# A decoder block's first stage with the contraction outside: features-first input, upper value tiles normalised late, the row factor through DRAM

## The chip, the cores and the metric

The kernel runs on one core of a Trainium2 chip. The metric is the device time of one execution in microseconds (us), as a median over repeated executions. The core has TensorE (PE: matmuls, and PEld: weight loads), VectorE (DVE), ScalarE (ACT), GpSimd (POOL) and SyncE (SP), which here only issues DMAs.

## The reference, cut to what matters

```python
h = rms_norm(x, norm1_g[l])                          # x: 1 x 1024 x 1024, float32
proj = jnp.einsum('bsd,dc->bsc', h, w_in[l])         # 1024 features -> q, k, v, pool, gates
q = proj[..., :c_q];  k = proj[..., c_q:c_k]         # 512 columns each
v = proj[..., c_k:c_v].reshape(B, S, 4, 128)         # 512 columns
...
q = rms_norm(q, q_norm_g[l]);  k = rms_norm(k, k_norm_g[l])
a = diff_attention(q, k, v, lam)                     # causal, 4 heads, two softmaxes a head
...                                                  # pooling mixer, gates, output projection
x = x + jnp.einsum('bsd,de->bse', merged, w_o[l])
u = jnp.square(jax.nn.relu(jnp.einsum('bsd,df->bsf', rms_norm(x, norm2_g[l]), w_mlp_in[l])))
x = x + jnp.einsum('bsf,fd->bsd', u, w_mlp_out[l])
```

`rms_norm` divides each row of x by the root of the mean of its squares (the reciprocal is called the row factor below) and multiplies each feature by its gain. There is one layer.

## The kernel before, in words

Every large product is done in three matmuls: both operands are split into a rounded part and the rest (`_hi` by a copy on ACT, `_lo` by a subtraction on DVE), and hi·hi, lo·hi and hi·lo are summed in PSUM (`passes`, L2299). One step of a contraction is thus three matmuls of 128x128 by 512 columns.

The first stage makes h transposed (`featT`, features on partitions, 8 blocks of 128 features by 1024 tokens, hi and lo), and from it v for all eight token tiles (`v_tok`). It goes token tile by token tile. For tile t: SP loads `x_tile` (128 tokens x 1024, L587); ACT squares it with a sum over the row (`x_square`, L1024); POOL turns the sum into the row factor (`inverse_root`, L948, two instructions); DVE multiplies by the factor and the gain (`x_norm`, L1507); PE transposes eight 128x128 blocks (`x_transpose`, L2312); ACT and DVE split them (`x_hi`, `x_lo`); PE multiplies with the value weights `v_w`, 24 matmuls (`v_project`, L2477; for tile 0 `v_first`); ACT and DVE split the result (`v_hi_part`, `v_lo_part`). The gain, one row, is spread over the partitions by matmuls with a single contraction row (L2506).

Two query-key projections follow among the last value tiles (`project`, 24 matmuls each, after tiles 5 and 6). Their rows are squared and copied by ACT (`qk_take`), summed (`qk_sum`), given a factor by POOL (`qk_inverse`), normalised (`qk_norm`), transposed on PE (`qk_transpose`, L2366) and split (`qk_hi`, `qk_lo`). Then the attention stage starts: `attend(0)` does three steps of the pool projection and then `scores(0)` (L2403, matmuls at L2422), which needs the split query and key tile 0. From there on PE has an order of work written out by hand, in which projections fill the places between the attention products, and later the gates, the output projection and the MLP follow.

Each engine runs its own list in the written order and waits on semaphores. SP's list is: x tile 0 in two halves, the value weights in four loads (`load_v_w`, L589), x tiles 1 and 2 among them, seven small loads for the vectors (L629 to L635), x tiles 3 and 4, the first query-key weights (`load_qk`, eight loads of 256 KB), x tiles 5 to 7, two loads for the pool projection.

Of the kernel before, what the change touches and what calls it, by code (L numbers as in the profile page):

```python
# [34 lines left out]
def trunk_layer(nc, x, norm1_g, w_in, b_gate, q_norm_g, k_norm_g, lam_params, subln_g,  # L35
                pool_w, pool_scale, w_up_attn, w_up_pool, w_o, norm2_g, w_mlp_in, w_mlp_out, y):
# [33 lines left out]
    with ExitStack() as ctx:  # L70
# [22 lines left out]
        g1_row = at("g1_row", 144, [P, D])  # L93
        h_row = [at(f"h_row{i}", 148 + 4 * i, [P, D]) for i in range(2)]
        square1 = at("square1", 156, [P, D])
        g_one = at("g_one", 208, [1, D])
# [7 lines left out]
        x_tile = [at(f"x_tile{i}", 128 + 4 * i, [P, D]) for i in range(4)]  # L104
        prob = [at(f"prob{c}", 144 + 4 * c, [P, SEQ]) for c in range(2)]
        w_tok = [at(f"w_tok{i}", 152 + 4 * i, [P, SEQ]) for i in range(2)]
        qk_square = [at(f"qk_square{i}", kb, [P, 8, HEAD]) for i, kb in enumerate((158, 118))]
# [85 lines left out]
        gate_store = nc.dram_tensor("gate_store", [2 * GP, P, SEQ], F32, kind="Internal").ap()  # L193
        res_store = nc.dram_tensor("res_store", [T, P, D], F32, kind="Internal").ap()
# [14 lines left out]
        vec_rows = at("vec_rows", 218, [N_ROWS, P])  # L209
# [9 lines left out]
        x_ss_half = sm(11)  # L219
# [22 lines left out]
        def sem(name):  # L242
# [4 lines left out]
        x_in = [sem(f"x_in{i}") for i in range(4)]  # L247
        res_in = [sem(f"res_in{i}") for i in range(3)]
# [5 lines left out]
        o_in = [[sem(f"o_in{i}_{j}") for j in range(4)] for i in range(2)]  # L254
        vec_in, g1_ready, g_in, x0_in, y_out = sem("vec_in"), sem("g1_ready"), sem("g_in"), sem("x0_in"), sem("y_out")

        zeroed, const_ready = sem("zeroed"), sem("const_ready")
        vec_full, col_ready, lam_step, lam_exped = (sem(n) for n in ("vec_full", "col_ready", "lam_step", "lam_exped"))

        w_hi, w_ready = sem("w_hi"), sem("w_ready")  # L260
        v_full, v_hi, v_ready = sem("v_full"), sem("v_hi"), sem("v_ready")

        x_squared, x_mean, x_inv, h_ready, xT_full, xT_hi, xT_split = (sem(n) for n in (
            "x_squared", "x_mean", "x_inv", "h_ready", "xT_full", "xT_hi", "xT_split"))
# [23 lines left out]
        gate_in = [sem(f"gate_in{i}") for i in range(4)]  # L288
# [73 lines left out]
        def qk_w(h2, piece):  # L362

            return (4 if h2 == 0 else 10) + piece + 1

        def x_w(g):

            return (9, 10, 15, 16)[g]
# [28 lines left out]
        def x_bank(t, b):  # L397

            return 2 * (t % 2) + b

        def v_bank(t):

            return POOLED + t % 2

        FIRST_W = 4 * HEADS + 1
# [75 lines left out]
        RAW_LOADS = (10, 10, 4, 4)  # L481
# [85 lines left out]

        def o_source(n):
# [14 lines left out]
        def _(sp):  # L583
            def load_x(t):

                wait(sp, h_ready, t - 2 if t > 3 else 0)
                sp.dma_start(x_tile[t % 4][:], x_rows[t]).then_inc(x_in[t % 4], 16)  # L587

            def load_v_w(i):  # L589

                src = w_in_v[:, 2 * i:2 * i + 2, V0:V0 + HEADS * P]
                sp.dma_start(k4(raw[i][:], 2), src).then_inc(raw_in[i], 16)
# [6 lines left out]
            def load_qk(h2, piece):  # L599

                r = piece if h2 == 0 else piece % 2
                sp.wait_ge(w_ready, piece + 1 if h2 == 0 else (9, 10, 11, 12)[piece])
# [5 lines left out]
            def load_pool_w(g):  # L608

                c0 = X0 + (GROUPS - 1 - g) * P  # L610
                load(g % 2, w_in_v[:, :, c0:c0 + P], (5, 6, 13, 14)[g], KD)
# [7 lines left out]
            sp.dma_start(x_tile[0][:, LOW], x_rows[0][:, LOW]).then_inc(x0_in, 16)  # L619
            sp.dma_start(x_tile[0][:, HIGH], x_rows[0][:, HIGH]).then_inc(x_in[0], 16)  # L620
            load_v_w(0)
            load_v_w(1)
            load_v_w(2)
            load_x(1)
            load_v_w(3)
            load_x(2)

            rows_of = lambda v: v.rearrange("l (j p) -> (l j) p", p=P)
            sp.dma_start(vec_rows[BG:PS, :], rows_of(b_gate)).then_inc(vec_in, 16)  # L629
            sp.dma_start(vec_rows[PS:SG, :], rows_of(pool_scale)).then_inc(vec_in, 16)  # L630
            sp.dma_start(vec_rows[SG:SG + 1, :], subln_g).then_inc(vec_in, 16)
            for r, g in ((QG, q_norm_g), (KG, k_norm_g)):
                for c in range(2):
                    sp.dma_start(vec_rows[r:r + 1, c * HEAD:(c + 1) * HEAD], g).then_inc(vec_in, 16)
# [3 lines left out]
            load_x(3)  # L638
            load_x(4)
            for piece in range(4):  # L640
                load_qk(0, piece)
            load_x(5)
            load_x(6)
            load_x(7)
# [18 lines left out]
            for p in range(4):  # L663
                if p == 2:
                    sp.wait_ge(pooled_full, 2 * GROUPS)
                load(p, gate_cols(2 * p, P), (15, 16, 16, 16)[p], KD)
# [168 lines left out]
            sp.dma_start(g2_row[:], norm2_g.to_broadcast([P, D])).then_inc(g_in, 16)  # L835
# [100 lines left out]
        def _(pool):  # L936
# [18 lines left out]
            def x_inverse(t, squared, mean, inv):  # L955
                inverse_root(x_ss[:, t:t + 1], D, x_ms[:, t:t + 1], x_rstd[:, t:t + 1], 1, squared, t + 1, mean, t + 1, inv)
# [26 lines left out]
            pool.wait_ge(x_squared, 1)  # L983
# [32 lines left out]
        def _(act):  # L1016
# [29 lines left out]
            def qk_hi(n):  # L1046

                act.wait_ge(tb_full, TB_USE["qk", n])
                if n == 0:
                    act.wait_ge(col_ready, 3)  # L1050
# [1708 lines left out]
```

## Time and profile before

| | |
|---|---|
| median of 3 runs | 1250.77 us (1250.71 to 1251.3) |
| span of the profiled execution | 1249.3 us |
| PE busy | 1240.8 us, 99% of the span |
| DVE busy | 937.9 us, 75% |
| ACT busy | 556.4 us, 45% |
| POOL busy | 141.4 us, 11% |
| DMA | 169.75 MB, mean 136 GB/s |
| first matmul of scores(0) | 76.32 us after the span's start |

The profiled execution has a span of 1249.3 us, from its first to its last instruction; the runs take 1.5 us more around it (1250.77 less 1249.3). Busy time of PE is a union of matmuls whose ends are modelled, and consecutive matmuls overlap: a row of 0.39 us for one matmul does not mean that it takes 0.39 us of the engine's time; the distance between starts tells that.

### The profile page before, as it was taken

The numbers are of one execution on the slowest core, as the hardware profiler recorded it, in microseconds if no ns is written. First come the engines' busy times: TensorE is split into PE (matmuls) and PEld (weight loads), VectorE is DVE, ScalarE is ACT, GpSimd is POOL, SyncE is SP. The second block draws the span as 40 slices with busy tenths as digits, with TensorE's granted clock in tenths as the row PEclk, the third lists the DMA queues.
The fourth block names the chain that finished last, engine by engine and source line by source line (L and its number), as shares of the span: only waits on it lengthen the run. The fifth ranks groups of instructions, "written<-read, shape, count | busy, mean of one in ns | idle before, by whom it ended". The sixth has DMA issues, their size and how long they took to land.

```text
span 1249.3 us, 16209 instructions
## 1 busy us (share of the span) xinstructions
PE 1240.8 (99%) x5885; PEld 1022.0 (82%) x5885; DVE 937.9 (75%) x1316; ACT 556.4 (45%) x961; POOL 141.4 (11%) x198
## 2 busy tenths in 40 slices
PE   9999999999999999999999999999999999999999
PEld 6878888887788888888887888888888888888887
DVE  5547786778987778754688778778679988879764
ACT  5436665666553324322345545445445333333330
POOL 2113223223300040000000000000000000000035
PEclk9999999999999999999999999999999999999999
DMA  7100120103375457332213553453569644363223
GB/s 274 35 17 16 58 60 19 38 23 106 127 261 177 144 188 267 119 117 86 100 65 129 170 175 123 160 173 112 176 240 363 218 158 167 102 236 102 101 95 141
DMA packets 110354, 169.75 MB, mean 136 GB/s; under 512 B 5806, under 2 KB 55875, under 8 KB 110276
## 3 DMA queue, kind: packets, MB, share of 16 engines
q1 hardware_dynamic: 110274, 168.72, 39.5%
q8 instruction: 47, 0.77, 0.2%
q14 instruction: 31, 0.25, 0.1%
q10 hardware_dynamic: 2, 0.00, 0.0%
HBM read 118.37 MB, written 50.33 MB: 135 GB/s over the span
## 4 chain that ended last, share of the span: by engine, by line
PE 89%; DVE 5%; ACT 3%; issue 2%; DMA 1%; SPq 0%; POOL 0%; ACTq 0%; DVEq 0%
PE bank L2301 81%; PE bank L2443 2%; PE bank L2422 2%; PE bank L2381 1%; DVE slot_lo L1504 1%; DMA x_tile<-in_x 1%; DVE c L2201 1%; DVE pair_lo L2095 1%; PE bank L2372 1%; PE bank L2658 1%; DVE small L1587 1%; DMA gate_store<-out_tile 1%; PE bank L2319 0%; ACT slot_hi L1022 0%; ACT prob L1067 0%
## 5 line engine op out<-in xcount | busy, mean ns | idle before, releaser
L2301 PE MATMUL bank<-o_hi,s_lo 128*128 128x512 f32 (+1 forms) x452 | 175.0, 387 | 0.0
L2301 PE MATMUL bank<-o_hi,s_hi 128*128 128x512 f32 (+1 forms) x452 | 175.0, 387 | 0.0
L2201 DVE TENSOR_TENSOR c<-bank,c 128x512 f32<-128x512 f32 x112 | 75.7, 688 | 35.6 <-PE bank L2301 33.9
L2301 PE MATMUL bank<-featT_hi,pair_hi 128*128 128x512 f32 x256 | 99.9, 390 | 0.7 <-DVE c L2201 0.6
L2301 PE MATMUL bank<-o_lo,s_hi 128*128 128x512 f32 (+1 forms) x260 | 100.3, 386 | 0.0
L2301 PE MATMUL bank<-featT_lo,pair_hi 128*128 128x512 f32 x256 | 99.6, 389 | 0.0
L2301 PE MATMUL bank<-featT_hi,pair_lo 128*128 128x512 f32 x256 | 99.6, 389 | 0.0
L2301 PEld LDWEIGHTS bank<-o_hi,s_hi 128*128 128x128 f32 x452 | 84.9, 188 | 17.5
L2301 PEld LDWEIGHTS bank<-o_hi,s_lo 128*128 128x128 f32 x452 | 84.9, 188 | 17.2
L1472 ACT ACTIVATE s_hi<-s_raw 128x2048 fp32r<-128x2048 f32 x28 | 53.7, 1917 | 94.6 <-DMA s_raw<-u_store 94.6
L1448 ACT ACTIVATE c<-c 128x512 f32<-128x512 f32 x64 | 39.9, 624 | 118.8 <-DVE c L2201 118.8
L2145 DVE TENSOR_TENSOR s_lo<-s_raw,s_hi 128x2048 fp32r<-128x2048 f32 x28 | 65.7, 2345 | 22.6 <-ACT s_hi L1472 22.5
L2301 PE MATMUL bank<-slot_hi,featT_hi 128*128 128x512 f32 x192 | 78.2, 407 | 0.0
L2301 PE MATMUL bank<-slot_lo,featT_hi 128*128 128x512 f32 x192 | 75.2, 391 | 0.0
L2301 PE MATMUL bank<-slot_hi,featT_lo 128*128 128x512 f32 x192 | 74.8, 390 | 0.0
L2301 PE MATMUL bank<-comb_hi,pair_hi 128*128 128x512 f32 x192 | 74.7, 389 | 0.0
L2301 PE MATMUL bank<-comb_hi,pair_lo 128*128 128x512 f32 x192 | 74.7, 389 | 0.0
L2301 PE MATMUL bank<-o_t_lo,s_hi 128*128 128x512 f32 x192 | 74.7, 389 | 0.0
L2301 PE MATMUL bank<-comb_lo,pair_hi 128*128 128x512 f32 x192 | 74.7, 389 | 0.0
L951 POOL TENSOR_SCALAR small<-small 128x1 f32<-128x1 f32 (+1 forms) x63 | 28.7, 456 | 392.3 <-ACT h_row L1434 169.3
L1006 POOL TENSOR_TENSOR p_acc<-p_acc,shared 128x512 f32<-128x512 f32 x4 | 5.2, 1291 | 570.0 <-DVE shared L2259 570.0
L2095 DVE TENSOR_TENSOR pair_lo<-pair_f,pair_hi 128x512 fp32r<-128x512 f32 x64 | 42.8, 688 | 30.0 <-ACT pair_hi L1422 28.8
(283 smaller groups left out, 3158.0 us busy)
## 6 DMA issues: line engine op xcount, KB each, us to landing
s_raw<-u_store SPq DMA_DIRECT2D x28, 1024.0 KB, 5.6
pair_raw<-in_w_mlp_in SPq DMA_DIRECT2D x16, 1024.0 KB, 5.9
u_store<-s_tile SPq DMA_DIRECT2D x64, 256.0 KB, 2.1
o_raw<-in_w_mlp_out SPq DMA_DIRECT2D x16, 1024.0 KB, 8.3
u_store<-u_tile SPq DMA_DIRECT2D x48, 256.0 KB, 2.4
gate_store<-out_tile SPq DMA_DIRECT2D x32, 256.0 KB, 2.6
gate_raw<-in_w_in SPq DMA_DIRECT2D x8, 1024.0 KB, 5.4
raw<-in_w_in SPq DMA_DIRECT2D x12, 512.0 KB, 4.8
```

The lines of the kernel that those rows point to most:

```text
L951: pool.tensor_scalar(ms, ss, 1.0 / n_mean, EPS, ALU.mult, ALU.add).then_inc(mean_sem, 1)
L1448: nc.scalar.activation(c[:], c[:], ACT.Relu).then_inc(relu_done, 1)
L1472: nc.scalar.activation(s_hi[n % 3][:], s_raw[n % 3][:], ACT.Copy).then_inc(d_hi, 1)
L1504: nc.vector.tensor_tensor(slot[1][:, 0:width], raw[r][:, 0:width], slot[0][:, 0:width], ALU.subtract).then_inc(w_ready, 1)
L1587: nc.vector.tensor_reduce(neg_max[u % 2][:, c:c + 1], score_view(u, c), AX.X, ALU.max, negate=True).then_inc(max_ready, 1)
L2095: nc.vector.tensor_tensor(pair_lo[par][:, i], src, pair_hi[par][:, i], ALU.subtract).then_inc(t_ready, 1)
L2145: nc.vector.tensor_tensor(s_lo[n % 3][:], s_raw[n % 3][:], s_hi[n % 3][:], ALU.subtract).then_inc(d_lo, 1)
L2201: nc.vector.tensor_tensor(out[:], psum, other[:], ALU.add).then_inc(up_sum, 1)
L2301: mm = nc.tensor.matmul(out, a, b, start=start and i == 0, stop=stop and i == len(steps) - 1, skip_group_check=onto)
L2372: mm = nc.tensor.transpose(bank[:, TB, i * P:(i + 1) * P], qk_row[n % 2][:, i * P:(i + 1) * P], ident[:])
L2422: mm = nc.tensor.matmul(bank[:, 2 * c + p0 // 512 if t >= 4 else 2 * j + c, 0:p1 - p0], a, b, start=i == 0, stop=i == 2)
L2443: mm = nc.tensor.matmul(*m, start=k == 0 and i == 0, stop=k == t and i == 1)
```

## The change

The host hands the kernel four more arrays, which hold the same numbers in another order: `v_and_high[k]` (for feature block k: 128 features x 512 value weights, and beside them x transposed for the upper 512 tokens), `x_low[k]` (x transposed for the lower 512 tokens), `g1_cols` (the gain, a feature per partition) and `vec_cols` (the other vectors, as columns). The x rows are still loaded, for the sums of squares alone.

- The transposes of x, their evictions, the spreading of the gain and the seven small loads go. `x_tile` is squared in place.
- The loop over k is outside and over four token tiles inside (`v_round(half, k)`): 12 matmuls for each k, with four PSUM banks open. First the upper half (tiles 4 to 7), on x times gain, without the row factor; v is multiplied by the factor when it is split. Then the lower half (tiles 0 to 3), on h.
- h needs the row factor along the free axis: four factors a partition are stored to DRAM as 512 numbers of 4 bytes (`rstd_store`), and loaded back, spread over 128 partitions (`spread`, 256 KB). SP waits for the store before it issues the load. DVE multiplies x by gain and `spread` (`norm_part`). The upper half is multiplied and split again (`norm_part(1, k)`, `h_lo_part(1, k)`), after the lower one, for all that comes later.
- Both query-key projections stand after the last value round.

```diff
+            def spread_rstd(half):
+                sp.wait_ge(x_inv, half + 1)
+                sp.dma_start(rstd_store[half].rearrange("(t p) -> p t", p=P),
+                             x_rstd[:, 4 * half:4 * half + 4], allow_slow_non_contiguous=True).then_inc(rstd_stored, 16)
+                sp.wait_ge(rstd_stored, 16 * (half + 1))
+                sp.dma_start(spread[:, HALVES[half]],
+                             rstd_store[half:half + 1].to_broadcast([P, HT])).then_inc(spread_in, 16)
...
+            sp.dma_start(front[0][:, HIGH], v_and_high[0][:, HIGH]).then_inc(high0_in, 16)
+            load_front(1)
+            load_x(0)
+            load_front(2)
             load_x(1)
+            load_front(3)
             load_x(2)
+            load_front(4)
+            load_x(3)
+            load_front(5)
+            load_qk(0, 0)
+            load_low(0)
+            load_front(6)
+            load_low(1)
+            load_front(7)
+            load_low(2)
+            load_qk(0, 1)
+            load_low(3)
+            spread_rstd(0)
+            for t in range(4, T):
+                load_x(t)
+            for k in range(4, KD):
+                load_low(k)
+            load_qk(0, 2)
+            load_qk(0, 3)
+            spread_rstd(1)
...
+            for half in range(2):
+                four = slice(4 * half, 4 * half + 4)
+                inverse_root(x_ss[:, four], D, x_ms[:, four], x_rstd[:, four], 4, x_squared, 4 * half + 4, x_mean, half + 1,
+                             x_inv)
...
+            act.dma_start(g1_col[:], g1_cols).then_inc(vec_in, 16)
+            act.dma_start(front[0][:, LOW], v_and_high[0][:, LOW]).then_inc(front_in[0], 16)
+            for k in range(KD):
+                plain_hi_part(k)
+                v_w_hi(k)
+                if 0 < k < 5:
+                    x_square(k - 1)
+                if k == 5:
+                    qk_weights_hi(0, 0)
+            qk_weights_hi(0, 1)
+            for k in range(KD):
+                h_hi_part(0, k)
+                if k < 4:
+                    x_square(4 + k)
+                elif k < 6:
+                    qk_weights_hi(0, k - 2)
+                elif k == 6:
+                    for t in range(4, T):
+                        v_hi_part(t)
+            for k in range(KD):
+                h_hi_part(1, k)
...
+            for k in range(KD):
+                plain_lo_part(k)
+                v_w_lo(k)
+                if k == 5:
+                    qk_weights_lo(0)
+            qk_weights_lo(1)
+            norm_part(0, 0)
+            for k in range(KD):
+                if k + 1 < KD:
+                    norm_part(0, k + 1)
+                h_lo_part(0, k)
+                if 3 < k < 6:
+                    qk_weights_lo(k - 2)
+                if k == 6:
+                    for t in range(4, T):
+                        v_lo_part(t)
+            norm_part(1, 0)
+            for k in range(KD):
+                if k + 1 < KD:
+                    norm_part(1, k + 1)
+                h_lo_part(1, k)
+            vectors()
+            for t in range(4):
                 v_lo_part(t)
+            qk_sum(0)
+            split_lo(x_w(0), 0, x_slot)
+            qk_norm(0)
+            qk_sum(1)
             qk_norm(1)
             qk_lo(0)
...
             pe.wait_ge(zeroed, 1)
+            for i in range(8):
+                nc.tensor.matmul(bank[:, v_bank(0), :], ones[:, 0:P].bitcast(F32R), ones[:].bitcast(F32R), start=True, stop=True)
+            for half in (1, 0):
+                for k in range(KD):
+                    v_round(half, k)
+            for n in range(2):
+                for k in range(KD):
+                    project(n, k)
             qk_transpose(0)
```

`load_front(k)` loads 512 KB (rows of 4 KB), `load_low(k)` 256 KB over the value weights of block k once they are split, `load_x(t)` 512 KB. `plain_hi_part` and `plain_lo_part` split x times gain, `v_w_hi` and `v_w_lo` the value weights, `h_hi_part` and `h_lo_part` h; each works on 128x512.

## Rows read from the trace of the kernel before

**Rows 1.** The page, part 1: busy time of PE, share of the span, instructions.

```profile
PE 1240.8 (99%) x5885; PEld 1022.0 (82%) x5885; DVE 937.9 (75%) x1316; ACT 556.4 (45%) x961; POOL 141.4 (11%) x198
```

**Rows 2.** Waits of PE over the whole span: us in total, times, longest.

```profile
PE bank L2443 <- DVE wT_lo L1570: 1.1, 2, 0.7
```

**Rows 3.** Groups of instructions, 0 to 75 us: count, busy us, mean ns of one.

```profile
L1027 ACT ACTIVATE square<-x_tile 128x1024 f32<-128x1024 f32 x7 | 7.5, 1064 | 0.6 <-DMA x_tile<-in_x 0.5
...
L1196 ACT ACTIVATE v_tok<-bank 128x512 fp32r<-128x512 f32 x8 | 4.8, 598 | 21.8 <-PE bank L2301 20.1 <-PE bank L2496 1.6
...
L1504 DVE TENSOR_TENSOR slot_lo<-raw,slot_hi 128x1024 fp32r<-128x1024 f32 x4 | 4.7, 1222 | 0.5 <-ACT slot_hi L1022 0.5
...
L953 POOL TENSOR_TENSOR small<-small 128x8 f32<-128x8 f32 x2 | 3.3, 1648 | 0.2
...
L1027 ACT ACTIVATION_READ_ACCUMULATOR square<-x_tile 128x1 f32 x7 | 1.4, 198 | 0.0
```

**Rows 4.** Timeline, start of the value products: start us, us, instruction.

```profile
9.03 2.14 PE L2496 MATMUL bank<-v_w_hi,featT_hi 128*128 128x512 f32 x4
```

**Rows 5.** Timeline, 74 to 77 us: the first stage's end.

```profile
74.25 0.69 DVE L1698 TENSOR_TENSOR v_tok<-bank,v_tok 128x512 fp32r<-128x512 f32 x1 [2.79 <-ACT v_tok L1196]
...
75.79 0.47 DVE L1563 SCALAR_TENSOR_TENSOR kT_lo<-bank,small,kT_hi 128x256 fp32r<-128x256 f32 x1
76.32 0.33 PE L2422 MATMUL bank<-kT_hi,qT_hi 64*128 64x128 f32 x2 [0.23 <-DVE kT_lo L1563]
```

**Rows 6.** Timeline of PE: first and last of 24 matmuls of project(0).

```profile
50.76 0.39 PE L2301 MATMUL bank<-slot_hi,featT_hi 128*128 128x512 f32 x1
...
55.97 0.39 PE L2301 MATMUL bank<-slot_lo,featT_hi 128*128 128x512 f32 x1
```

**Rows 7.** Timeline of PE: two neighbouring matmuls near the start, and a later pair.

```profile
11.40 0.63 PE L2496 MATMUL bank<-v_w_lo,featT_hi 128*128 128x512 f32 x1
11.82 0.63 PE L2496 MATMUL bank<-v_w_hi,featT_lo 128*128 128x512 f32 x1
...
13.34 0.63 PE L2496 MATMUL bank<-v_w_lo,featT_hi 128*128 128x512 f32 x2
```

**Rows 8.** The very first load (256 KB, issued at 0.72): issue to landing.

```profile
DMA to landing us min/median/max: 2.5/2.5/2.5
```

**Rows 9.** Single loads of 512 KB: the issue, then its landing.

```profile
L592 SPq DMA_DIRECT2D raw<-in_w_in x1: 427/427/427, 1.6 to 1.6; - x1
DMA to landing us min/median/max: 5.2/5.2/5.2
...
L592 SPq DMA_DIRECT2D raw<-in_w_in x1: 469/469/469, 2.1 to 2.1; - x1
DMA to landing us min/median/max: 6.7/6.7/6.7
...
L587 SPq DMA_DIRECT2D x_tile<-in_x x1: 863/863/863, 4.5 to 4.5; - x1
DMA to landing us min/median/max: 9.5/9.5/9.5
...
L587 SPq DMA_DIRECT2D x_tile<-in_x x1: 432/432/432, 8.6 to 8.6; - x1
DMA to landing us min/median/max: 7.8/7.8/7.8
```

**Rows 10.** A store of 128 KB (attn_store) at 148.5 us, no load in flight: landing.

```profile
DMA to landing us min/median/max: 2.1/2.1/2.1
```

**Rows 11.** Timeline of DVE: first and last instruction of vectors().

```profile
45.55 0.28 DVE L1527 TENSOR_TENSOR lam_prod<-lam_in 128x128 f32<-128x128 f32 x1
...
47.09 0.15 DVE L1541 TENSOR_SCALAR small<-col 128x1 f32<-128x1 f32 x1
```

**Rows 12.** Windows at the end: busy us, then PEclk, the granted clock.

```profile
1246.00:1247.00 1.00, 0.74 (x7) 0.54 (x5) 0.22 (x1) 0.00 (x0) 0.00 (x0) 1.00 0.50 175
...
1248.00:1249.00 1.00, 0.00 (x0) 0.00 (x0) 0.00 (x0) 0.00 (x0) 0.00 (x0) 0.86 0.39 131
```

More of the change, by code:

```diff
@@ L92, in trunk_layer @@
         v_w = both("v_w", 96, [P, KD, HEADS * P], 16)
[L93 to L96, printed above, removed]
+        front = [at(f"front{k}", 128 + 4 * k, [P, D]) for k in range(KD)]
+        x_tile = [at(f"x_tile{i}", kb, [P, D]) for i, kb in enumerate((72, 80, 88, 208))]
+        spread = at("spread", 64, [P, SEQ])
         ones = at("ones", 212, [P, HT])
@@ L601, in load_qk @@
                 r = piece if h2 == 0 else piece % 2
-                sp.wait_ge(w_ready, piece + 1 if h2 == 0 else (9, 10, 11, 12)[piece])
+                wait(sp, w_ready, 0 if h2 == 0 else (5, 6, 7, 8)[piece])
                 for i, c0 in enumerate((0, K0)):
@@ L1114, in qk_weights_hi @@
                 r = piece if h2 == 0 else piece % 2
-                loads = 3 if h2 == 0 else 6 + 2 * (piece // 2)
+                loads = 2 if h2 == 0 else 5 + 2 * (piece // 2)
                 used = () if h2 == 0 else (qk_full, T)
@@ L2501, in _ @@
-            pe.wait_ge(zeroed, 1)
-            for i in range(4):
-                nc.tensor.matmul(bank[:, v_bank(1), :], ones[:, 0:P].bitcast(F32R), ones[:].bitcast(F32R), start=True, stop=True)
-            pe.wait_ge(g_in, 16)
-            for i, half in enumerate((LOW, HIGH)):
-                nc.tensor.matmul(bank[:, (TB, OUT)[i], :], ones[0:1, 0:P], g_one[:, half], start=True,
-                                 stop=True).then_inc(vec_full, 1)
-            pe.wait_ge(const_ready, 1)
-            x_transpose(0)
@@ L2525, in _, with v_round @@
-            v_project(1, range(4, 8))
-            for t in range(2, T):
-                if t + 1 < T:
-                    x_transpose(t + 1)
-                v_project(t, range(4))
-                v_project(t, range(4, 8))
-                if t == 2:
-                    pe.wait_ge(vec_in, 16 * 8)
-                    nc.tensor.transpose(bank[:, OUT, 0:N_ROWS], vec_rows[:],
-                                        ident[0:N_ROWS, 0:N_ROWS]).then_inc(vec_full, 1)
-                if t in (5, 6):
-                    for k in range(KD):
-                        project(t - 5, k)
+            def v_round(half, k):
+                tiles = range(4, T) if half == 1 else range(4)
+                for i, (a, b) in enumerate(((0, 0), (1, 0), (0, 1))):
+                    if half == 1:
+                        pe.wait_ge((plain_hi, plain_split, v_w_ready)[i], k + 1)
+                        if i == 0:
+                            pe.wait_ge(v_w_rounded, k + 1)
+                    elif i < 2:
+                        pe.wait_ge((h_hi, h_split)[i], k + 1)
+                    for t in tiles:
+                        mm = nc.tensor.matmul(bank[:, v_bank(t), :], featT[a][:, k, columns(t)], v_w[b][:, k, :],
+                                              start=k == 0 and i == 0, stop=k == KD - 1 and i == 2)
+                        if k == KD - 1 and i == 2:
+                            mm.then_inc(v_full, 1)
@@ L2754 @@
         args.append(nc.dram_tensor(f"in_{name}", a.shape, mybir.dt.from_np(a.dtype), kind="ExternalInput").ap())
+    columns = np.asarray(inputs["x"]).reshape(1024, 8, 128).transpose(1, 2, 0)
+    v_rows = np.asarray(inputs["w_in"]).reshape(8, 128, -1)[:, :, 1024:1536]
+    vectors = [np.asarray(inputs["b_gate"]).reshape(-1), np.asarray(inputs["pool_scale"]).reshape(-1),
+               np.asarray(inputs["subln_g"]).reshape(-1)]
+    for name in ("q_norm_g", "k_norm_g"):
+        vectors.append(np.tile(np.asarray(inputs[name]).reshape(-1), 2))
+    laid_out = {
+        "v_and_high": np.concatenate([v_rows, columns[:, :, 512:]], axis=2),
+        "x_low": columns[:, :, :512],
+        "g1_cols": np.asarray(inputs["norm1_g"]).reshape(8, 128).T,
+        "vec_cols": np.concatenate(vectors).reshape(-1, 128).T,
+    }
+    for name, a in laid_out.items():
+        a = np.ascontiguousarray(a)
+        arrays[f"in_{name}"] = a
+        args.append(nc.dram_tensor(f"in_{name}", a.shape, mybir.dt.from_np(a.dtype), kind="ExternalInput").ap())
     args.append(nc.dram_tensor("out_y", inputs["x"].shape, F32, kind="ExternalOutput").ap())
```

337 lines of the change are left out of this document (119 added, 218 removed).

## The prediction, made before the change was run

> **What bounds the kernel now.** I read the page first: PE is busy 99% of the span [rows 1]. The waits of PE over the whole span come next: the longest single wait behind another engine is 0.7 us [rows 2]. So what is won before the attention stage reaches the end of the kernel whole, if PE's later work stays as it is, and it does: the diff leaves the order from `attend(0)` on alone. The quantity to forecast is therefore one instant, the start of scores(0), at 76.32 us [rows 5]. Then I read the timeline of the first 77 us. The pace of PE comes from project(0): 24 matmuls start between 50.76 and 55.97, 23 distances, so 0.2265 us each [rows 6]. Near the start the distance is 0.42 us [rows 7], as at the lower of the clock's two levels (1.2 GHz), though the granted clock in the page reads full there. From about 13.1 us the pace is the faster one: a pair at 13.34 takes 0.63 us in all, 0.39 for the last and 0.24 between the starts [rows 7]. Before scores(0), PE must do 192 value and 48 projection matmuls, 54.4 us at the faster pace. So 76.3 - 54.4 = 21.9 us are something else: the late start (first value matmul at 9.03 [rows 4]), the slow pace, the 64 transposes of x, and the handover at the end, where scores(0) starts 0.06 us after DVE's last split (75.79 + 0.47) [rows 5].
>
> **What the change removes and adds on PE.** The 64 transposes go. Eight warming matmuls stand ahead instead of four and the four gain matmuls. The 240 matmuls remain, so PE's floor is its start plus 54.4 us plus its pauses. What decides is when data come, so I follow the loads.
>
> **When loads land.** The first load of 256 KB takes 2.5 us and lands at 3.2 [rows 8]. On the one queue the loads land in order: issued at 1.6, 2.1, 4.5 and 8.6 they land at 6.85, 8.8, 14.0 and 16.4 [rows 9]. They close 1.0, 1.5, 3.5 and 4.0 MB (of 1024 KB) of the queue. From 8.8 to 14.0 that is 2 MB, 1.30 us for each 512 KB. From 14.0 to 16.4 it is 1.1 us more, with the seven small loads in between. The new list has, to `load_low(3)`, 8.0 MB. With the same start and 1.30 us a half MB: front(1) closes 1.0 MB and lands at 6.85, front(2) (2.0) at 10.1, front(3) at 12.7, x tile 3 (4.5) at 16.6, front(7) (7.0) at 23.1, low(3) (8.0) at 25.7.
>
> A page speaks against this rate. The Trainium skill, DMA: Bandwidth & Descriptors, Specifications, gives one core some 358 GB/s of HBM, where the rows show 512 KB in 1.30 us, 403 GB/s. By the page each half MB would take 1.46 us, and the forecast below would come out 2.7 us later, at 1248.2. The measured pair is from this very stretch, so I keep 1.30.
>
> **The upper half.** ACT splits 128x512 in 0.60 us [rows 3]. Round 0 has both hi parts at about 5.0 (load of the weights half at some 4.4, one split). Round 7 has them at 23.1 + 1.2 = 24.3. PE takes 12 x 0.42 = 5.1 us for round 0, to 10.1. If the slow pace lasts to 13.1 as before, round 1 ends at 14.3, and six more at 2.72 us end at 30.6; no load is later than that. DVE and ACT have 1.2 and 2.5 us of work in each 2.7, so nothing queues there.
>
> **The factor's way through DRAM** is the new wait. The fourth square (ACT 1.06 + 0.20 [rows 3]) ends at 17.9 and POOL's two instructions at about 19.3 (its power over 8 columns takes 1.65 [rows 3]; over 4 I take 1.1). SP then issues the store, but 3 MB still stand in the queue ahead of it, so it can't land before 25.7. For its 512 numbers of 4 bytes the trace has no row. An idle queue lands 128 KB in 2.1 us [rows 10], and a store behind others overlaps most of that, so the lower bound is 0.3 us. The upper bound is the small loads' 1.1 us for 155 rows scaled to 512: 3.6 us. I take 1.5, nearer to the small loads: 27.2. SP waits for it; behind SP stand x tiles 4 to 7, low(4) to low(7), the query-key weights 2 and 3. The spread load then takes 2.5 as the first one did [rows 8], with 0.1 to notice: 29.8. Bounds 28.6 to 31.9.
>
> **The lower half.** DVE normalises block 0 (0.65), ACT splits it (0.60): PE starts at 31.2, a pause of 0.6. x tile 7 lands at 35.0 and weights 2 and 3 at 38.9 and 40.2. PE needs 96 x 0.2265 = 21.8 us, to 53.0, and 10.9 for the two projections, to 63.9. DVE has much more than before. A 128x512 step is half of 1.22 us [rows 3], 0.61. Block 4 waits for ACT, which must do four squares (1.2 each) and five splits first: it ends at 38.9. From there DVE is in line: weights 2 to 41.2, blocks to 42.4, weights 3 to 43.6, to 44.9, four value splits at 0.69 [rows 5] to 47.6, the last block to 48.3, the upper half's 16 steps (9.8) to 58.1, `vectors()` 1.7 [rows 11] to 59.8, four value splits to 62.5, the first sum to 63.2. The pool weights wait for ACT (63.8) and end at 65.0. POOL's factor (0.2 + 1.65) is there at 65.1; qk_norm(0) ends at 65.8, qk_sum(1) at 66.5, POOL at 68.4, qk_norm(1) at 69.1, the split at 69.9. Each of some 17 handovers between ACT and DVE costs 0.06 [rows 5], 1.0 in sum: scores(0) starts at 71.0. PE alone would be ready at 63.9 + 4.7 (square, sum, factor, norm, split) = 68.6, so DVE sets the end, by 2.4 us. If DVE's steps were free, that is all there would be to win.
>
> **The sum.** 76.3 - 71.0 = 5.3 us earlier. The profiled span of 1249.3 becomes 1244.0. The runs take 1.5 us more than it (1250.77), so 1245.5 us. The upper half's second normalising, 9.8 us of DVE, stands on the path though PE doesn't need it until scores(0); the transposes, the late start and the small loads pay for it.
>
> **Rivals.**
> *The loads stay slow* (the slower side). Between 6.85 and 8.8 a half MB took 1.95 us [rows 9]. The new list moves 4 MB more than the old one before the attention stage, and both x tile 7 and the factor's store hang on the queue. 17 half MBs lie between 8.8 and x tile 7, each 0.65 later: 11.1 us, scores(0) at 82.1, 1256.6 us. The gain is gone at 1.61 us a half MB, and it is slower by over 0.2% from 1.76 us. For it: more bytes, and x read twice. Against: the old list held 1.30 with the same mixture of sizes. Chance 0.10.
> *The clock falls in a pause.* At the end of the kernel the granted clock falls between 1248 and 1249, after the last matmul in the window 1246 to 1247 [rows 12], so some 2 us of idleness can be enough. The new order has pauses that the old one has nowhere [rows 2]: 0.6 at 30.6, and 2.2 at 63.9, between the projections and the transpose, and 2 before scores(0). Near the start the slow pace held through 4.1 us of value matmuls, 9.03 to 13.1, and cost 4.1 x (1 - 0.2265/0.42) = 1.9 us. The first fall would be hidden by DVE's slack of 2.4 us; one after 64 is paid in full: 1247.4. Chance 0.15. The Trainium skill, TensorE: Matmul & The Clock Gate, HAM oscillation, says the same of kernels that wait between bursts: the engine comes back at half the clock. By that rule the time is the 1247.4 of this rival, without it 1245.5.
> *The store passes the queue.* Landed 2.1 us after its issue at 19.3 [rows 10], the factor is spread at about 24.2, no pause is left, PE ends at 63.3, and scores(0) starts about 68.4 with handovers: 1242.9. Against: loads issued at 8.6 waited 7.8 us for those ahead [rows 9]. Chance 0.08.
> *The shift isn't passed on*, since the first attention rows wait for DVE, ACT or late weights rather than PE: between 0 and 2.5 us faster, about 1249.5. Rows 2 speak against it. Chance 0.07.
>
> **How the numbers follow.** My forecast has 0.60. A measurement of this kernel tells from no change about 0.2%, 2.5 us, so faster means under 1248.3 and slower over 1253.3. Forecast, passing store and most of the clock's case are faster: 0.76. Between lie the untransmitted shift, part of the clock's case and a mild slowing of the loads: 0.15. Slower: 0.09. The store's bounds give 1244.3 to 1247.6 and the clock's case adds 1.9, to 1249.5. The passing store sets the lower end with its error: 1242. Range 1242.0 to 1249.5.
>
> **What the profile of the changed kernel would show.** front(7) lands near 23 and low(3) near 26, the spread load near 30. PE pauses little between the halves and 2 us before `qk_transpose(0)`; ahead of scores(0) stands DVE's split, and DVE is busy without a break from 39 to 65. Wrong would be: x tile 7 after 38, a spread load before 26 or after 33, scores(0) behind anything but DVE, or a distance of 0.42 us between matmuls after 64.

## The result, and the profile after

| | before | changed |
|---|---|---|
| median | 1250.74 us (1250.31 to 1251.3, 4 runs) | 1258.58 us (1257.97 to 1260.66, 4 runs) |
| span of the profiled execution | 1249.3 us | 1258.8 us |
| first matmul of scores(0) | 76.32 us | 84.57 us |

The ratio is 1.0063 (95% interval 1.0049 to 1.0078): slower by 0.6%, where 0.4% faster was forecast. The profiled execution of the changed kernel is its slowest (1260.66 us). In it scores(0) starts 8.25 us later than before, and the medians differ by 7.84. What follows scores(0) takes 1174.2 us (1258.8 less 84.57) against 1173.0. So most of the loss lies ahead of the attention stage, and here the shift of that start reaches the end.

The page of the changed kernel, part 1, then the granted clock of part 2. PE is busy 6.8 us less than in [rows 1], and the second and third slices (31.5 to 94.4 us) have a reduced clock.

```profile
PE 1234.0 (98%) x5820; PEld 1018.7 (81%) x5820; DVE 943.4 (75%) x1334; ACT 562.0 (45%) x969; POOL 135.8 (11%) x186
...
PEclk9889999999999999999999999999999999999999
```

The two long waits of PE, 0 to 90 us (in total, times, longest). Before, the longest was 0.7 us [rows 2], but for 1.3 us behind POOL ahead of PE's first matmul, which the prediction's reading of these rows leaves out.

```profile
PE bank L2399 <- DVE qk_row L1594: 7.4, 1, 7.4
PE bank L2516 <- ACT featT_hi L1074: 7.1, 1, 7.1
```

L2516 is the value matmul: PE stands between the upper and the lower half. L2399 is the query-key transpose. Behind both stands DVE, whose longest wait from 25 to 65 us is this:

```profile
DVE front L1554 <- DMA spread<-rstd_store: 15.5, 2, 10.2
```

And behind DVE stands SP (its waits from 15 to 60 us). It waited 20.5 us for its own two stores to land.

```profile
SPq L615 <- DMA rstd_store<-small: 20.5, 2, 12.5
```

The single issues of the first half, store and then load:

```profile
L612 SPq DMA_DIRECT2D rstd_store<-small x1: 370/370/370, 17.3 to 17.3; - x1
DMA to landing us min/median/max: 12.9/12.9/12.9
...
L615 SPq DMA_DIRECT2D spread<-rstd_store x1: 339/339/339, 30.2 to 30.2; - x1
DMA to landing us min/median/max: 5.9/5.9/5.9
```

Those of the second half:

```profile
L612 SPq DMA_DIRECT2D rstd_store<-small x1: 366/366/366, 46.5 to 46.5; - x1
DMA to landing us min/median/max: 8.4/8.4/8.4
...
L615 SPq DMA_DIRECT2D spread<-rstd_store x1: 338/338/338, 54.9 to 54.9; - x1
DMA to landing us min/median/max: 6.0/6.0/6.0
```

Was the first store held by the loads ahead of it? The windows tell (busy us of each engine, then the granted clock, the DMA share, GB/s): from about 24 us there is almost no traffic.

```profile
22.00:24.00 2.00, 2.00 (x10) 1.67 (x9) 1.35 (x2) 1.05 (x3) 0.00 (x0) 1.00 0.99 279
24.00:32.00 8.00, 6.52 (x29) 5.07 (x27) 1.22 (x1) 0.69 (x1) 0.00 (x0) 1.00 0.01 2
...
34.00:36.00 2.00, 0.00 (x0) 0.00 (x0) 0.00 (x0) 0.00 (x0) 0.00 (x0) 0.62 0.97 230
```

The traffic of the loads ends at 24, the store lands at 30.2 (17.3 + 12.9), and in those 6.2 us almost nothing moves (16 KB between 26 and 27). The last load ahead of the store, low(3), is late too: issued at 14.0, it lands after 13.7 us, at 27.7, where it lands between 24.1 and 24.5 in every kernel below that has no store or one without 4-byte writes side by side. Nobody waits for it here. The same in the view of DMA traffic, 0 to 90 us in 40 slices of 2.25 us (tenths of the engines' time, then GB/s): two holes, one for each trip. The page's chain of work that ended last names the store too: `DMA rstd_store<-small 2%`.

```profile
DMA  1999999999600049999941100399200000160000
GB/s 23 340 405 415 417 415 395 377 401 373 170 7 0 0 39 219 404 410 397 358 153 1 7 0 0 44 229 313 68 0 0 0 0 0 16 217 0 0 0 0
```

The timeline at the end of the first hole, and those of PE and DVE before scores(0):

```profile
36.16 1.42 DVE L1554 SCALAR_TENSOR_TENSOR front<-front,g_col,spread 128x512 f32<-128x512 f32 x2 [10.22 <-DMA spread<-rstd_store]
...
37.63 1.22 PE L2516 MATMUL bank<-v_w_hi,featT_hi 128*128 128x512 f32 x2 [7.11 <-ACT featT_hi L1074]
...
79.68 1.12 PE L2399 MATMUL bank<-ident,qk_row 128*128 128x128 f32 x4 [7.40 <-DVE qk_row L1594]
...
83.20 0.47 DVE L1602 SCALAR_TENSOR_TENSOR kT_lo<-bank,small,kT_hi 128x256 fp32r<-128x256 f32 x1
83.58 0.63 PE L2341 MATMUL bank<-featT_hi,x_slot_lo 128*128 128x512 f32 x1
84.01 0.63 PE L2341 MATMUL bank<-featT_lo,x_slot_hi 128*128 128x512 f32 x1
84.57 0.47 PE L2450 MATMUL bank<-kT_hi,qT_hi 64*128 64x128 f32 x2
```

After the second pause the matmuls start 0.43 us apart (83.58, 84.01), not 0.23. DVE's last split ends at 83.67 (83.20 + 0.47), and PE has no gap between 79.68 and 84.57: scores(0) starts 0.9 us after DVE's split because PE, at the lower pace, has not finished the nine pool matmuls ahead of it. Before, it started 0.06 us after the split [rows 5].

### The profile page after: what moved, and what is told of

The parts are those of the page before. It is cut to its first block, busy times and chain, and to the rows that moved or that the text cites. A ratio compares the mean times of both kernels' runs of the same rounds, so it can differ in the third digit from the quotient of the medians.

```text
span 1258.8 us, 16093 instructions
## 1 busy us (share of the span) xinstructions
PE 1234.0 (98%) x5820; PEld 1018.7 (81%) x5820; DVE 943.4 (75%) x1334; ACT 562.0 (45%) x969; POOL 135.8 (11%) x186
## 4 chain that ended last, share of the span: by engine, by line
PE 84%; DVE 6%; DMA 4%; ACT 3%; issue 2%; POOL 0%; SPq 0%; DVEq 0%; ACTq 0%
PE bank L2341 77%; PE bank L2471 2%; PE bank L2450 2%; DMA rstd_store<-small 2%; DMA x_tile<-in_x 1%; PE bank L2408 1%; PE bank L2399 1%; DVE c L2241 1%; DVE pair_lo L2135 1%; DVE slot_lo L1536 1%; PE bank L2650 1%; DVE small L1626 1%; DMA spread<-rstd_store 0%; ACT x_tile L1053 0%; POOL small L980 0%
## 5 line engine op out<-in xcount | busy, mean ns | idle before, releaser
L2241 DVE TENSOR_TENSOR c<-bank,c 128x512 f32<-128x512 f32 x112 | 75.7, 688 | 35.3 <-PE bank L2341 33.6
L978 POOL TENSOR_SCALAR small<-small 128x1 f32<-128x1 f32 (+2 forms) x58 | 25.7, 443 | 410.3 <-ACT h_row L1466 169.3
```

The source lines that it names most:

```text
L978: pool.tensor_scalar(ms, ss, 1.0 / n_mean, EPS, ALU.mult, ALU.add).then_inc(mean_sem, 1)
L2241: nc.vector.tensor_tensor(out[:], psum, other[:], ALU.add).then_inc(up_sum, 1)
```

## The experiments

Each is an edit of the changed kernel unless said otherwise. The kernel before took, in the same series and on the same chip as each, 1251.4 us (e1 to e4), 1251.3 (e5, e6, e7, e10), 1251.2 (e8, e9) and 1250.62 (e11, e12).

### Without the store, and with another load

```diff
# e1_no_store
-                sp.dma_start(rstd_store[half].rearrange("(t p) -> p t", p=P), ...).then_inc(rstd_stored, 16)
-                sp.wait_ge(rstd_stored, 16 * (half + 1))
-                sp.dma_start(spread[:, HALVES[half]], rstd_store[half:half + 1].to_broadcast([P, HT]))
+                sp.dma_start(spread[:, HALVES[half]], x_rows[half][0:1, LOW].to_broadcast([P, HT]))
# e2_plain_load: the store stays
+                sp.dma_start(spread[:, HALVES[half]], x_rows[half][:, LOW])
```

> The factor's store to DRAM and the wait for it go; SP still waits for the factors, then spreads 512 numbers of x's first row in their place (so h is scaled by wrong numbers, the work is the same). Theory (the two trips through DRAM set the end: 12.9 and 8.4 us from the store's issue to its landing, of which PE pays a pause of 7.1 us between the halves and DVE one of 5.3 us before the upper half): the spread load then stands in the queue at 17.4 and lands by 30, PE's pause falls under 1 us, DVE's goes, scores(0) starts 9 to 11 us earlier than 84.6, and the time is 1247 to 1250. Rival (the clock is what costs: two falls): the pauses shrink but at most 4 us come back, 1254 or more. Rival (DVE's chain sets the end whenever the factors come): only DVE's own 5.3 us come back, 1253.

Measured: 1244.93 us (1243.72 to 1244.96), ratio 0.9947 (0.9932 to 0.9961). scores(0) starts at 67.94; there is no pause between the halves. The traffic has no hole:

```profile
DMA  1999999999999997687000000002500000000000
```

So all of the loss, and more, hangs on the store and its wait; the time is below the 1247 to 1250 of the theory. Without the store the kernel is 6.5 us under the one before, where 5.3 were forecast for the change.

It could be more, for scores(0) starts 8.4 us earlier. What follows it takes 1175.3 us here (1243.2 less 67.94) against 1173.0 before. The window from 70 to 75 us shows where time is lost, first here and then in e11 (the last experiment), where the clock stays high and what follows scores(0) takes 1173.5:

```profile
70.00:75.00 5.00, 5.00 (x19) 4.02 (x18) 0.74 (x3) 0.61 (x4) 0.00 (x0) 0.71 0.00 0
```

```profile
70.00:75.00 5.00, 5.00 (x28) 3.83 (x27) 2.24 (x8) 1.62 (x7) 0.00 (x0) 1.00 0.00 0
```

> The store and the wait stay; the load behind them reads 128 rows of x (256 KB) where the changed kernel reads one row of 2 KB 128 times (again wrong numbers, same work). Theory that reading one row 128 times is slow (5.9 us to landing, packets of 2048 bytes that take several times as long): landing in 2.5 to 3 us, both trips 3 us shorter, scores(0) 5 to 6 us earlier, 1252 to 1254. Rival (the store's landing is all of it and 5.9 us is the price of any load after an idle stretch): no change, 1258.

Measured: 1255.84 us (1255.36 to 1257.19), ratio 1.004 (1.0025 to 1.0054), scores(0) at 79.89. The stores land after 12.9 and 8.2 us as in the changed kernel. The loads land after 4.3 and 4.7, in place of 5.9 and 6.0. The load of one row to all partitions is thus a part of the loss (2.7 us of the medians), the store the larger. Each trip is 1.6 and 1.5 us shorter, not 3, and the time stays above the theory's 1252 to 1254.

### The same store in runs of 16 bytes

```diff
# e3_store16
-                sp.dma_start(rstd_store[half].rearrange("(t p) -> p t", p=P), ..., allow_slow_non_contiguous=True)
+                sp.dma_start(rstd_store[half].rearrange("(p t) -> p t", t=4), ...)
...
+                by_tile = spread[:, HALVES[half]].rearrange("p (q t) -> p t q", t=4)
                 # norm_part multiplies by by_tile: reads 16 bytes apart
```

> The store writes 128 runs of 16 bytes in place of 512 of 4 (DRAM holds the four factors of a partition side by side, and DVE reads the spread factors in steps of 16 bytes). Theory that the number of small writes sets the 6 to 8 us between the last packet and the landing: landing within 3 us of the queue's end, scores(0) 7 to 9 us earlier if DVE's stepped read costs nothing, 1249 to 1252. Rival (a fixed price of a store's receipt): less than 1 us, 1257 to 1259. If DVE's read in steps is slower, its 16 instructions leave 0.75 us each and the profile shows it.

Measured: 1250.96 us (1250.19 to 1251.34), ratio 0.9996 (0.9987 to 1.0006). The first store lands at 24.4, with the queue, the second 1.4 us after its issue:

```profile
L612 SPq DMA_DIRECT2D rstd_store<-small x1: 338/338/338, 40.0 to 40.0; - x1
L615 SPq DMA_DIRECT2D spread<-rstd_store x1: 339/339/339, 41.4 to 41.4; - x1
DMA to landing us min/median/max: 1.4/3.4/5.3
```

The spread is there at 29.6, as forecast (29.8). But DVE pays for the stepped read, and scores(0) starts at 75.26. The group from 25 to 75 us:

```profile
L1555 DVE SCALAR_TENSOR_TENSOR front<-front,g_col,spread 128x512 f32<-128x512 f32 x16 | 18.1, 1144 | 3.7 <-DMA spread<-rstd_store 3.7
```

In the changed kernel the same 16 instructions take 747 ns each, 6.3 us less in all. The Trainium skill, SBUF — State Buffer, Specifications (TRN2), speaks of 16-byte cachelines, and of a penalty for each access that crosses into a new line. Every number of this read lies 16 bytes from the last, and the 1144 against 747 ns agree.

### Useless matmuls in the pauses

```diff
# e4_warm: 28 matmuls ahead of the lower half, 30 ahead of qk_transpose(0)
+            def warm(n, b):
+                for i in range(n):
+                    nc.tensor.matmul(bank[:, b, :], v_w[0][:, 0, 0:P], v_w[0][:, 0, :], start=True, stop=True)
```

> 28 and 30 matmuls of no use in the two pauses of PE (30.4 to 37.6, 71.9 to 79.7), nothing else. Theory (trips through DRAM): the clock's falls cost only what stands on PE's path after 79.7: half pace from 79.7 to 85.7, some 2 to 3 us; the first fall is hidden by DVE, so 1255 to 1257. Rival (the clock is what makes the change slower): 1251 or less.

Measured: 1258.86 us (1257.91 to 1260.2), ratio 1.0061 (1.0046 to 1.0076): as slow as the changed kernel. The granted clock, though, stays high, first in the changed kernel and then in this one:

```profile
30.00:40.00 10.00, 2.89 (x9) 1.99 (x8) 2.77 (x4) 2.20 (x4) 0.00 (x0) 0.72 0.72 220
...
70.00:80.00 10.00, 2.60 (x13) 1.87 (x12) 7.75 (x17) 5.76 (x11) 2.69 (x2) 0.77 0.14 40
80.00:90.00 10.00, 10.00 (x45) 7.91 (x44) 3.29 (x10) 1.56 (x6) 1.84 (x2) 0.72 0.03 12
```

```profile
30.00:40.00 10.00, 6.51 (x28) 5.02 (x27) 2.77 (x4) 2.20 (x5) 0.00 (x0) 0.95 0.74 195
...
70.00:80.00 10.00, 10.00 (x47) 8.27 (x46) 7.32 (x15) 5.19 (x11) 2.97 (x4) 1.00 0.17 52
80.00:90.00 10.00, 9.29 (x53) 7.43 (x52) 4.23 (x12) 2.31 (x8) 1.57 (x1) 1.00 0.01 2
```

scores(0) starts at 83.07, 1.5 us earlier than in the changed kernel. Of these, 0.7 are not the clock's: the second factors came that much earlier in this execution (DVE starts on the upper half at 60.18, not 60.86). The other 0.8 are, since scores(0) now starts 0.06 us after DVE's last split and not 0.9. The medians show nothing of it (the interval of the ratio is 3.8 us wide), and the theory's 1255 to 1257 was missed. The clock's falls are there, but they are not the cause of the loss.

### The factors put in order by ACT

```diff
# e5_in_order: on e3_store16, norm_part as in the changed kernel
+                act.wait_ge(spread_in, 16 * (half + 1))
+                nc.scalar.activation(spread[:, HALVES[half]].rearrange("p (t q) -> p t q", q=P),
+                                     mixed[:].rearrange("p (q t) -> p t q", t=4), ACT.Copy)
```

> As e3_store16 (128 runs of 16 bytes), but ACT puts the spread factors in order by one copy a half, so that DVE reads them side by side. In e3 the 16 multiplications took 1.14 us each instead of 0.75, 6.3 us on DVE's chain. Theory (trips through DRAM, then DVE's chain): the factors in order at about 30.5, scores(0) at 69.5 to 71, 1244.5 to 1247, which is what the prediction gave for the change itself. Rival (what lies after the trip is bound by something else than DVE): no better than e3_store16, 1250 to 1251.

Measured: 1248.03 us (1246.2 to 1248.43), ratio 0.9971 (0.996 to 0.9983). scores(0) starts at 71.49; the forecast had 71.0. The time is 1 us above the theory's 1247 all the same: what follows scores(0) takes 1174.9 us, with a granted clock of 0.50 from 74 to 76. The six executions differ in the same way. The one with a mean clock of 1.000 over the whole span took 1246.2 us, the one with 0.999 took 1246.86, the four with 0.997 took 1247.82 to 1248.43. DVE's one wait for the factors is 5.0 us, PE's pause between the halves 4.2, since the upper half ended at 28.1 in this execution.

### The factors spread by PE

```diff
# e6_pe_spread: no store, no load
+                for t in range(4):
+                    pool.tensor_scalar(diag[:, t * P:(t + 1) * P], ident[:],
+                                       x_rstd[:, 4 * half + t:4 * half + t + 1], None, ALU.mult)
...
+                nc.tensor.matmul(bank[:, (0, 3)[half], :], ones[:, 0:P], diag[:], start=True, stop=True)
# not shown: ACT copies the bank to spread; norm_part(0, 0) ahead of qk_weights_lo(1); upper values evicted at k == 4
# e7_split_first: e6, and qk_lo(0) ahead of qk_norm(1); e10_before_order: that exchange alone, in the kernel before
```

> No DRAM: POOL builds diagonal matrices of the factors, one float32 matmul with ones spreads them into a PSUM bank, ACT copies it out. The upper values are evicted two steps earlier so that a bank is free for the second half. Theory: no pause between the halves, DVE's chain starts by 25, scores(0) at 66 to 68, 1242.5 to 1245, and about 1 us under e1_no_store at best. Rival (PE's added matmuls and the earlier evictions cost what the load cost): as e5_in_order.

Measured: 1247.53 us (1247.08 to 1248.99), ratio 0.9972 (0.996 to 0.9983), scores(0) at 72.28: outside the theory's 66 to 68, with a time like that of e5, as the rival had it, though not for the rival's reason. PE has no pause between the halves. But the second spread comes only when PE reaches it in its order, between value rounds 5 and 6, and DVE waits 4.57 us for it. Timeline of DVE:

```profile
49.37 1.42 DVE L1558 SCALAR_TENSOR_TENSOR front<-front,g_col,spread 128x512 f32<-128x512 f32 x2 [4.57 <-ACT spread L1069]
```

> As e6_pe_spread, and DVE splits the first query-key tile before it waits for the second tile's factor. Theory (DVE's list at the end of the stage sets scores(0)): 2 us earlier, 1240.5 to 1243. Rival (PE sets it by then): under 0.5 us.

Measured: 1247.39 us (1245.7 to 1247.84), ratio 0.9968 (0.9957 to 0.998), scores(0) at 72.09: 0.2 us earlier, where the theory had 2. This order of DVE's is not the cost.

> The kernel before with that same exchange alone: the first split before the second normalising. The split then starts 0.6 us earlier at most, and PE has 0.23 us of idleness before scores(0): theory 0.2 us, not to be told from nothing, 1250.5 to 1251.5. Rival (the exchange is worth 2 us in any kernel): 1249.

Measured: 1251.15 us (1250.48 to 1251.91), ratio 0.9999 (0.999 to 1.0009): nothing.

### What of the store is slow: number or closeness of the writes

All three are e2_plain_load with another store; the load reads x in each.

```diff
# e8_spaced: 512 numbers, 512 bytes apart;  e12_sixteen: s=16, 64 bytes apart
+                sp.dma_start(rstd_store[half].rearrange("(t p s) -> s p t", p=P, s=128)[0], ...)
# e9_quarter: 128 numbers, side by side
+                sp.dma_start(rstd_store[half, 0:P].rearrange("(t p) -> p t", p=P), x_rstd[:, 4 * half:4 * half + 1], ...)
```

> On e2_plain_load (the load doesn't need what is stored): the same 512 numbers of 4 bytes, each 512 bytes from the next in DRAM. Theory (each small write is slow by itself, so their number counts): issue to landing of the second store stays at about 8 us. Rival (writes to one stretch of 2 KB wait for each other): under 3 us, as the 128 runs of 16 bytes with 1.4.

Measured, one run: 1246.62 us (before 1251.2). The first store lands at 24.5, with the queue's end (24). Single issues, second store and second load:

```profile
L612 SPq DMA_DIRECT2D rstd_store<-small x1: 366/366/366, 37.0 to 37.0; - x1
DMA to landing us min/median/max: 2.4/2.4/2.4
...
L615 SPq DMA_DIRECT2D spread<-in_x x1: 341/341/341, 39.4 to 39.4; - x1
DMA to landing us min/median/max: 2.7/2.7/2.7
```

> On e2_plain_load: only one of a partition's four factors is stored, 128 numbers of 4 bytes side by side (three quarters of the store are left out; the load doesn't need them). Theory (number of small writes): the second store lands in 2.5 to 3.5 us, a quarter of the 6 to 7 us above the floor. Rival (any write of 4 bytes brings the same wait): 8 us.

Measured, one run: 1252.58 us (before 1251.2). The stores land after 12.4 and 6.8 us, the loads after 4.5 and 3.9: neither the theory's 2.5 to 3.5 nor the rival's 8.

> The run with the plain load, with the same 512 numbers of 4 bytes stored 64 bytes apart (4 bytes apart in the changed kernel, 512 bytes apart in the spaced run); the load reads other rows, so the factors are not the reference's. It asks how close two small writes must be to delay each other. If only writes to the same 64 bytes do, the second store lands after about 2.4 us, as at 512 bytes. If all within 512 bytes do (8 numbers in place of 128 share such a stretch), it lands between, after some 2.7 to 4 us; if what counts is the number of writes to one partition of 2 KB, likewise. If the delay has nothing to do with closeness but with the total stretch of memory, it lands between 2.4 and 8.2 us in proportion. Time 1246.6 if it lands at 2.4.

Measured, one run: 1245.54 us (before 1250.62). The first store lands at 24.5 again. The second store:

```profile
L612 SPq DMA_DIRECT2D rstd_store<-small x1: 367/367/367, 37.3 to 37.3; - x1
DMA to landing us min/median/max: 2.3/2.3/2.3
```

The number isn't it: with a quarter of the writes the store lands 1.4 us sooner than the 8.2 of e2, and all 512 of them at a distance take 2.3 to 2.4. Nor is it the size of one write alone, which is 4 bytes in all four runs. It is closeness: at 4 bytes apart 8.2 us, at 64 or 512 bytes 2.3 and 2.4. These are single runs, but each has two stores and both say the same. Where between 4 and 64 bytes the step lies wasn't tried. Nor was it tried whether closeness is enough: neighbouring numbers come from different partitions here, and no run writes neighbours of 4 bytes from one partition. And the load behind the store pays as well: the same load, of other memory, takes 4.3 and 4.7 us behind the close writes and 2.5 to 2.7 behind the spaced ones.

The Trainium skill, DMA: Bandwidth & Descriptors, Specifications, asks for 512 B or more in a transfer for the full rate, and says that below it the engine does read-modify-write. No run here shows such reads. The trace agrees that small writes side by side are slow, but being under 512 B is not enough: 4-byte writes 64 bytes apart landed in 2.3 us, 16-byte runs in 1.4 and 2.7.

### Each half's factors by the way that suits it

```diff
# e11_mixed_ways: e7_split_first for the lower half; for the upper half, at the end of SP's loads:
+                sp.dma_start(rstd_store[1].rearrange("(p t) -> p t", t=4), x_rstd[:, 4:8]).then_inc(rstd_stored, 16)
+                sp.wait_ge(rstd_stored, 16)
+                sp.wait_ge(spread_full, 1)
+                sp.dma_start(mixed[:], rstd_store[1:2].to_broadcast([P, HT])).then_inc(spread_in, 16)
# and ACT's copy that orders them, as in e5_in_order
```

> The changed kernel with each half's factor brought its own way: for the lower half four diagonals on POOL and one matmul against ones (as in the run with the matmul spread), for the upper half the 16-byte store, the load, and one copy on ACT that puts the factors in order (as in the run in order). The second spread no longer waits for PE's place in its list. My theory (DVE's chain sets scores(0), and what held DVE were the two waits for a spread): the store is issued near 39.6 and lands 1.4 us later, the load 5 us after that, near 46.5, so DVE's idle 4.5 us before the second normalising shrink to under 1, scores(0) starts at 67.9 to 69 (72.09 with both on PE, 67.94 without any store) and the time is 1244.9, 0.5% under the kernel before. Rival: PE's own end sets it, as the gap of 3.5 us ahead of the query-key transpose is the square, sum and factor of the last projection: then scores(0) stays at 71 or later and the time at 1247.

Measured: 1242.1 us (1241.73 to 1242.14), ratio 0.9931 (0.9915 to 0.9948), scores(0) at 66.83. The store is issued at 33.6, not 39.6, and lands after 2.7 us. PE's waits in the first 90 us are three, two of them at the start:

```profile
PE bank L2537 <- ACT v_w_hi L1075: 1.7, 1, 1.7
PE bank L2544 <- POOL ones L965: 1.3, 1, 1.3
PE bank L2429 <- DVE kT_lo L1623: 0.3, 1, 0.3
```

The granted clock is 1.00 from 60 to 80 us. This kernel beats the one before by 0.7%, where the changed one lost 0.6%. It is also better than my theory's 1244.9: with both waits gone, DVE's chain ends so early that PE has no pause ahead of the transpose and goes through from the projections to the scores. Against e1, scores(0) starts 1.1 us earlier and what follows is 1.8 us shorter. The rival, that the last projection's square and sum set the end, falls.

## Why the prediction was wrong, step by step

| instant, us | forecast | changed | e1, no store | e11 |
|---|---|---|---|---|
| store landed, lower half | 27.2 | 30.2 | none | none |
| DVE starts on the lower half | 29.8 | 36.2 | 26.1 | 24.0 |
| DVE starts again on the upper half | 48.3 | 60.9 | 44.7 | 44.6 |
| scores(0) | 71.0 | 84.6 | 67.9 | 66.8 |

**The first view and the question were right in the main.** The start of scores(0) decides most of it: what follows keeps its length within 1.2 us in the changed kernel. It is not a rule: in e1, e5 and e8 what follows is 1.9 to 2.3 us longer than before.

**The loads were right up to the store.** front(7) was forecast at 23.1 and landed at 21.4; low(3) was forecast at 25.7, and the queue's traffic ended at 24. The lower rate of the Trainium skill, DMA: Bandwidth & Descriptors, Specifications, wasn't met here either (windows of 382 and 392 GB/s between 14 and 22 us); the page gets it by halving a stack's 716 GB/s between two cores, and here one core runs. The upper half ended at 30.5 against 30.6. That the loads stay slow falls as a rival; the time near its 1256.6 is a coincidence.

**The step that failed is the price of the store's landing**, "an idle queue lands 128 KB in 2.1 us [...] so the lower bound is 0.3 us. The upper bound is [...] 3.6 us. I take 1.5". It is 6.2 us behind the end of the queue's traffic, outside both bounds. The prediction compared with transfers of large pieces ([rows 10]) and with small loads by their number. Neither row has writes of 4 bytes side by side, and e8, e9 and e12 show that this property makes the price. e3 shows the rest of the step sound: with 16-byte runs the spread is there at 29.6.

**"The spread load then takes 2.5 as the first one did"** was off by 3.4 us (5.9). e2 and e8 divide this: 1.6 for reading one row to all partitions rather than 128 rows (5.9 against 4.3), 1.8 for what the store leaves behind (4.3 against 2.5). With no store (e1) the load of one row takes 3.4, so the two parts don't simply add up. Together: 6.2 - 1.5 + 5.9 - 2.5 - 1.7 for the queue that ended earlier = 6.4, the whole of 36.2 - 29.8.

**The second trip was not costed at all.** The prediction has no term for it, so it took these factors as ready before 48.3. SP issues the second store only at 46.5. Its list stood for 12.5 us behind the first one and all later loads with it, so x tile 7 landed only at 42.3; ACT's square of it ended at 44.3 and POOL's factor at 46.5. The trip then takes 14.4 us. DVE would have been free at 55.6 (60.86 less its 5.27 us of idleness) and got the factors at 60.9: 5.3 us. This is one cause paid twice: once on the path and once through the queue behind it.

**DVE's chain** was nearly right. The multiplying steps take 747 ns and the splits 688 (610 was taken), but neighbours overlap: a pair starts every 1.27 us, 0.63 a step. From the first factor to the upper half it would have been 19.4 us against 18.5. From the upper half to DVE's last split it is 22.8 us, and to scores(0) 23.7, against 22.7. So this last 1.0 is almost all the lower clock's: scores(0) comes 0.9 us after the split and not 0.06. The sum of what is off: 6.4 + 0.9 + 5.3 + 1.0 = 13.6 us, which is 84.6 - 71.0 in the profiled execution; by the medians the time is 13.1 us above the forecast.

**The rivals.** The clock does fall after both pauses, as its rival says. The Trainium skill, TensorE: Matmul & The Clock Gate, HAM oscillation, says so of waits between bursts, and the granted clock of 0.72 from 80 to 90 us agrees. In the changed kernel it costs some 0.9 us ahead of scores(0), of 8. It costs more where the long waits are gone: in e1 and e5 what follows scores(0) is 1.9 to 2.3 us longer than before, near the 1.9 that this rival was priced at. That the clock makes this difference is argued from the windows and from the six executions of e5; no run holds the clock up in e1 or e5 and changes nothing else. "The store passes the queue" (1242.9, scores(0) at 68.4) did not happen, but e1 shows what it would have been worth: 67.9 and 1244.9. The range's upper end of 1249.5 was too low since the store's bounds were too narrow, and because the second half had no bound at all.

**All four signs named beforehand appeared.** x tile 7 landed at 42.3, not by 38; the spread load landed at 36.1, after 33; scores(0) stood behind PE's slow matmuls and not behind DVE; and matmuls started 0.43 us apart after 64. All four follow from the wait for the store.

## What to carry to other kernels

Before a value makes a round trip through DRAM, look at the pattern of its writes: lay out neighbouring small values as runs of 16 bytes or further apart, or spread them with a matmul, and price store and load by a row with the same pattern, with a wide upper bound if there is none. A wait for a landing on an issuing queue delays every later issue; cost the second trip with the first one's delay in it, and put such waits at the end of the list. A step moved off PE's path pays fully only when the engine that takes it over never waits ahead of it: with one wait for the factors left, the new order gave 3.3 us (e5) and 3.8 (e6), with none 6.5 (e1), and 8.5 (e11) where PE had no pause either. Look also behind the instant that you forecast: it can come earlier and the time follow only in part.

## What the hardware showed unexpectedly

- 512 writes of 4 bytes side by side landed 6.2 us after the loads' traffic had ended, and 8.2 to 8.7 us after an issue to a queue with little in it; 64 or 512 bytes apart 2.3 and 2.4; 128 side by side 6.8; 128 runs of 16 bytes 1.4 (e3) and 2.7 (e11).
- A load of 256 KB issued 3.4 us ahead of the close writes landed late as well: at 27.7 us in the changed kernel, 30.0 in e2, 28.3 in e4, against 24.1 to 24.5 in e1, e3, e5, e8 and e12. In e9, with 128 close writes, it landed at 24.2.
- A load of 256 KB behind the close writes took 4.3 to 4.7 us, behind spaced ones 2.5 to 2.7, though it read other memory (4.5 and 3.9 behind the 128 close writes of e9). Of the same kind is that the load of rstd_store took 5.3 us in the upper half of e3 and 4.7 in that of e5, where the 16-byte store had landed after 1.4, and 3.3 in e11, where it had landed after 2.7 (e1, without any store: 3.4). Store and load together take 6.7, 6.1 and 6.0. Why is open.
- A DVE multiplication whose second operand is read in steps of 16 bytes takes 1144 ns against 747.
- The granted clock fell to the lower level after pauses of PE of 7.1 and 7.4 us, in e5 after 4.2. In e1 it fell after two short pauses (0.5 us before 63.55, 1.7 us before 67.94) and when PE was already at work again: 0.88 from 68 to 70, 0.50 from 70 to 72.
